# First query and key tiles of three attention branches made in the gate stage, and the threshold rows spread over three merges

## What is computed

```python
def token_mixer(x, w_in, b_forget, sinks, w_branch, w_gate, b_gate, w_out):
    ...
    (aq, ak, av, bq, bk, bv, cq, ck, cv, ciq, cik, ciw, dq, dk, dv, df) = jnp.split(x @ w_in, offsets, axis=-1)
    ...
    o_a, _, _ = banded_attention(...)      # window of 128, sinks
    o_b = dilated_attention(...)           # three dilations
    o_c = dsa_attention(...)               # the 256 best keys of each query by an indexer's score
    o_d = forgetting_attention(...)        # a bias from cumulative forget gates
    branches = jnp.stack([o.reshape(b, L, BRANCH_WIDTH) for o in (o_a, o_b, o_c, o_d)], axis=2)
    proj = jnp.einsum('bsnk,nkd->bsnd', branches, w_branch)
    gates = jax.nn.sigmoid(x @ w_gate + b_gate).reshape(b, L, N_BRANCH, D_MODEL)
    merged = jnp.sum(gates * proj, axis=2)
    return merged @ w_out
```

## Time and profile before

| | us |
|---|---|
| median of three runs (2091.12 to 2094.64) | 2093.48 |
| the profiled execution | 2093.97 |
| its span, first to last instruction | 2092.2 |
| TensorE busy | 2060.4 |
| VectorE busy | 1536.4 |
| ScalarE busy | 968.5 |
| GpSimd busy | 937.3 |

### The profile page before, as it was taken

How to read it: one execution, slowest core, us unless ns; L and a number is a source line. 1 busy time by engine, 2 the same in 40 slices (tenths; PEclk the granted TensorE clock), 3 DMA queues, 4 the chain that set the end, 5 groups by cost and what they waited for, 6 DMA issues and landing times.

```text
span 2092.2 us, 28999 instructions
## 1 busy us (share of the span) xinstructions
PE 2060.4 (98%) x10382; PEld 1727.0 (83%) x10382; DVE 1536.4 (73%) x2549; ACT 968.5 (46%) x1740; POOL 937.3 (45%) x796
## 2 busy tenths in 40 slices
PE   9999999999999999999999999999999999999998
PEld 7788888888888888888888888888788888888887
DVE  8678887777686666797785666668877777775668
ACT  5543334566615556615635666523433333344540
POOL 4287752333322223324523333524756565645651
PEclk9999999999999999999999999999999999999999
DMA  4233323110042111230031000441566665558862
GB/s 132 72 111 110 101 91 62 31 31 21 26 152 64 50 32 51 75 100 28 22 121 31 21 21 11 141 161 61 180 181 203 191 192 161 171 189 310 270 215 92
DMA packets 197373, 224.26 MB, mean 107 GB/s; under 512 B 25704, under 2 KB 149608, under 8 KB 197232
## 3 DMA queue, kind: packets, MB, share of 16 engines
q1 hardware_dynamic: 194320, 212.43, 32.7%
q10 hardware_dynamic: 2912, 10.00, 1.3%
HBM read 164.17 MB, written 58.23 MB: 106 GB/s over the span
## 4 chain that ended last, share of the span: by engine, by line
PE 87%; DVE 7%; issue 2%; ACT 2%; POOL 1%; DMA 0%; DVEq 0%; ACTq 0%; POOLq 0%
PE pair L1359 13%; PE pair L927 13%; PE pair L911 7%; PE pair L1225 7%; PE obank L1359 5%; PE pair L1388 5%; PE obank L1021 4%; PE chunk L1000 4%; PE pair L1318 3%; PE chunk L1388 3%; PE obank L1225 3%; PE pair L972 3%; PE pair L973 3%; PE pair L1271 2%; PE obank L1388 2%
## 5 line engine op out<-in xcount | busy, mean ns | idle before, releaser
L2175 POOL TENSOR_TENSOR w_lo<-w_raw,w_hi 128x1024 fp32r<-128x1024 f32 x64 | 159.5, 2492 | 311.1 <-ACT w_hi L1652 311.0
L1675 ACT ACTIVATE pt_hi<-chunk 128x512 fp32r<-128x512 f32 (+1 forms) x272 | 150.8, 555 | 179.2 <-PE chunk L1000 177.8
L2578 DVE TENSOR_TENSOR pt_lo<-chunk,pt_hi 128x512 fp32r<-128x512 f32 (+1 forms) x272 | 173.2, 638 | 80.1 <-ACT pt_hi L1675 75.7
L2230 POOL TENSOR_SCALAR prob<-prob,att 128x256 f32<-128x256 f32 (+4 forms) x172 | 118.1, 696 | 198.5 <-DVE att L2514 198.2
L927 PE MATMUL pair<-act_hi,w_hi 128*128 128x512 f32 x432 | 186.4, 432 | 2.5 <-DVE heads L2519 2.3
L927 PE MATMUL pair<-act_hi,w_lo 128*128 128x512 f32 x432 | 170.0, 393 | 0.0
L927 PE MATMUL pair<-act_lo,w_hi 128*128 128x512 f32 x432 | 169.4, 392 | 0.0
L2399 DVE TENSOR_SCALAR_CACHE_REDUCE o_top<-score,stat 128x384 uint8<-128x384 f32 (+1 forms) x186 | 167.0, 941 | 0.5
L1021 PE MATMUL obank<-pt_hi,heads 128*128 128x256 f32 (+1 forms) x568 | 148.4, 285 | 0.6 <-DVE pt_lo L2578 0.6
L1777 ACT ACTIVATE prob<-prob,att 128x257 f32<-128x257 f32 (+6 forms) x172 | 120.5, 702 | 39.3 <-DVE att L2504 38.0
L1021 PE MATMUL obank<-pt_lo,heads 128*128 128x256 f32 (+1 forms) x568 | 138.6, 281 | 0.0
(11 more groups left out here) (489 smaller groups left out, 5932.5 us busy)
## 6 DMA issues: line engine op xcount, KB each, us to landing
down_sums<-dn_sums SPq DMA_DIRECT2D x40, 512.0 KB, 6.4
w_raw<-in_w_in SPq DMA_DIRECT2D x37, 512.0 KB, 3.8
gates<-o_t SPq DMA_DIRECT2D x22, 512.0 KB, 2.9
up_raw<-in_w_up SPq DMA_DIRECT2D x22, 512.0 KB, 4.8
gate_raw<-in_w_ffn_gate SPq DMA_DIRECT2D x22, 512.0 KB, 6.0
hidden<-gelu_s SPq DMA_DIRECT2D x22, 512.0 KB, 3.3
dn_raw<-down_sums SPq DMA_DIRECT2D x44, 256.0 KB, 4.1
h_in<-down_sums SPq DMA_DIRECT2D x44, 256.0 KB, 4.8
```

The source lines that it names most:

```text
L2175: nc.gpsimd.tensor_tensor(split_into(1, g), w_raw[:, g % 2, 0:kt * cols], split_into(0, g).bitcast(F32), ALU.subtract).then_inc(lo_ready, 1)
L2578: nc.vector.tensor_tensor(pt_lo[:, n % PT_SLOTS, 0:m], t[:, 0:m], pt_hi[:, n % PT_SLOTS, 0:m].bitcast(F32), ALU.subtract).then_inc(chunk_f ...
```

## The change

The six first query and key tiles of D, A and C are appended to the gate tiles (`HEAD_TILES`) and go through the gate stage as three more pairs, copied in place of the sigmoid and stored to `heads_dram`. The gate stage has 14 pairs in place of 11, and `TOPK_GATES` 15 search parts a pair; the whole search, and the counts of larger scores, end there (197 parts). The rows of distances (five parts each) lie in three merges: three rows in B's, two in D's, one in A's.

The projections at the start of D, A and C are gone. In their place is a step `heads`: SP loads V's weights, the two stored tiles into `o_t` rows 0 and 1, D's first two forget biases, and gate tiles 6 and 7 of the branch before, whose homes are now those of tiles 4 and 5. ScalarE and VectorE split the first query and the first key in halves of 512 tokens from `o_t`, then the second ones; the last gate tile of the merge is gated after the first halves (in C after the first two biased scores). TensorE goes from the merge to the V projection, in C to transposes of the stored tile and filler parts (`FIRST_C`), and waits for `first_placed` before the scores that need a half. ScalarE's split of the next weights moves from behind the merge and the projections to between the first two exponentials (in C behind its query splits).

```diff
-TOPK_GATES = {1: 2, 6: 2, 2: 2, 5: 2, 7: 2, 3: 2, 4: 2}
-TOPK_MERGE = {B: (2, 3), D: (1, 2), A: (0, 1), C: (0, 0)}
-TOPK_FIRST = {("k", D): 7, ("q", D): 6, ("k", A): 5, ("q", A): 5}
-SEARCH_PARTS = 191
-DISTANCE_PARTS = 6
+TOPK_GATES = {1: 3, 6: 2, 2: 2, 5: 2, 7: 2, 3: 2, 4: 2}
+SEARCH_PARTS = 191 + NSC
+DISTANCE_PARTS = 5
+MERGE_ROWS = {B: 3, D: 2, A: 1}
+MERGE_PARTS = {B: (8, 2), D: (4, 1), A: (3, 1)}
...
 
-BESIDE_C = (((0, 0), (0, 2), (1, 1), (1, 1), (2, 2), (3, 0), (3, 1), (6, 0), (6, 2), (8, 1),
+BESIDE_C = (((0, 0), (3, 0), (3, 1), (6, 0), (6, 2), (8, 1),
              (10, 1), (11, 2), (12, 2), (14, 0), (17, 2), (18, 2), (20, 2), (21, 1),
              (21, 2)),
...
 EARLY_GATES = {NKT - 3: 4, NKT - 2: 5, NKT - 1: 7}
-FIRST_C = 4
+FIRST_C = (4, 5)
 
 FILLER_GATES = [(B, 1), (B, 2), (B, 3)]
 STORED_GATES = {B: range(1, NKT), A: range(1, NKT), D: range(1, NKT), C: range(1, NKT - len(EARLY_GATES))}
-GATE_TILES = [(br, dt) for br in BRANCH_ORDER for dt in STORED_GATES[br] if (br, dt) not in FILLER_GATES]
+HEAD_TILES = [(what, br) for br in BRANCH_ORDER[1:] for what in ("q", "k")]
+GATE_TILES = [(br, dt) for br in BRANCH_ORDER for dt in STORED_GATES[br] if (br, dt) not in FILLER_GATES] + HEAD_TILES
 NGATE = len(GATE_TILES) // 2
 assert len(GATE_TILES) == 2 * NGATE
...
     for nb, br in enumerate(BRANCH_ORDER):
-        if br == C:
-            out += [("kv_c",)]
-        if br == A:
-            out += [("k", A, 0)]
-        out += [("q", br, 0)]
-        if br in (B, D):
-            out += [("k", br, 0)]
+        out += [("q", br, 0), ("k", br, 0)] if br == B else [("heads", br)]
         out += [("v_c",)] if br == C else [("v", br, 0)]
         out += [("attn", br, pr) for pr in range(PAIRS)]
         out += [("osplit", br), ("merge", br, nb == 0)]
...
-            tile = prob if n % 2 or n == NGATE - 1 else w_raw
+            tile = prob if n % 2 else w_raw
...
+            if tile not in HEAD_TILES:
+                return w_tile(w_gate[0], tile[0] * D_MODEL + tile[1] * P, P)
+            what, br = tile
+            return w_tile(w_in[0], Q_COL[br] if what == "q" else CK if br == C else K_COL[br], P)
+
+        def tile_kept(tile):
+
+            return heads_dram[HEAD_TILES.index(tile)] if tile in HEAD_TILES else gates_dram[tile]
...
+        def first_head(what):
+
+            return o_t[:, 0 if what == "q" else 1, :]
...
-            return dt % 2 if br == FINAL and dt >= 4 else dt % GATE_HOMES
+            if br == FINAL:
+                return dt % 2 if dt >= 4 else dt
+            return dt if dt < GATE_HOMES else dt - 2
...
-                    fill(FIRST_C)
+                    fill(FIRST_C[0])
+                    pe.wait_ge(first_placed, placed_first(br, 1))
                     scores(br, pr, 0)
                     scores(br, pr, 1)
+                    fill(FIRST_C[1])
...
+                        if p == 0 and br != B and u in (4, 8):
+                            pe.wait_ge(first_placed, placed_first(br, u // 4 + 1))
...
                         pe.wait_ge(chunk_free, chunk_base[1])
+                        if pr == 0 and merge_tiles.n:
+                            pe.wait_ge(merge_free, merge_tiles.n)
...
-                if merge_tiles.n and kind in ("q", "k", "kv_c", "outproj"):
+                if merge_tiles.n and kind in ("v", "v_c", "outproj"):
                     pe.wait_ge(merge_free, merge_tiles.n - 1)
-                elif merge_tiles.n and kind in ("v_c", "attn"):
-                    pe.wait_ge(merge_free, merge_tiles.n)
...
+                    if step[1] != B:
+                        pe.wait_ge(first_placed, placed_first(step[1], 1))
                     scores(step[1], step[2], 0)
...
-                    pe.wait_ge(pair_free[1], tiles[1].n)
-                    transpose_tokens(staged)
+                    pe.wait_ge(heads_loaded, 32 * len(BRANCH_ORDER[1:]))
+                    transpose_tokens(first_head("k"))
...
+            def load_heads(br):
+
+                at = BRANCH_ORDER.index(br) - 1
+                if at == 0:
+                    sp.wait_ge(merge_free, 4)
+                else:
+                    sp.wait_ge(sum_done, sums_of(BRANCH_ORDER[at]) + 4)
+                for what in ("q", "k"):
+                    tile = GATE_TILES.index((what, br))
+                    sp.wait_ge(gate_stored[tile % 2], 16 * (tile // 2 + 1))
+                    sp.dma_start(first_head(what), tile_kept((what, br))).then_inc(heads_loaded, 16)
...
-                    sp.wait_ge(merge_free, merge_at(br) + dt - GATE_HOMES + 1)
+                    sp.wait_ge(merge_free, merge_at(br) + dt - 1)
                 else:
-                    sp.wait_ge(sum_done, sums_of(br) + (1 if br == FINAL else dt - GATE_HOMES + 1))
+                    sp.wait_ge(sum_done, sums_of(br) + (1 if br == FINAL else dt - 1))
...
+                if step[0] == "heads":
+                    for source in ring_sources(("v", step[1], 0)) if step[1] != C else ():
+                        load_weights(source)
+                    load_heads(step[1])
+                    if step[1] == D:
+                        forget_bias(0)
+                        forget_bias(1)
+                    for dt in range(GATE_HOMES, NKT):
+                        load_gate_tile(BRANCH_ORDER[BRANCH_ORDER.index(step[1]) - 1], dt)
                 for n, source in enumerate(ring_sources(step)):
-                    if step in (("q", B, 0), ("k", B, 0)):
+                    if step in (("q", B, 0), ("k", B, 0), ("v", D, 0), ("v", A, 0)):
                         continue
...
-                        if n < NGATE - 3:
+                        if n < NGATE - 2:
...
-                            br, dt = GATE_TILES[2 * n + k]
-                            sp.dma_start(gates_dram[br, dt], gate_out[k]).then_inc(gate_stored[k], 16)
+                            sp.dma_start(tile_kept(GATE_TILES[2 * n + k]), gate_out[k]).then_inc(gate_stored[k], 16)
...
+                if tile in HEAD_TILES:
+                    return nc.scalar.activation(dst, src, ACT.Copy)
+                return nc.scalar.activation(dst, src, ACT.Sigmoid, bias=gate_bias_of(*tile))
...
+            def first_heads(br):
+
+                at = BRANCH_ORDER.index(br)
+                act.wait_ge(merge_full, NKT * at)
+                act.wait_ge(heads_loaded, 32 * at)
+                first_half(br, 0)
+
+            def first_half(br, s):
+
+                q_hi(br, 0, 0, first_head("q")[0:HD, half_cols(s)], half_cols(s))
+                k_hi(0, first_head("k")[0:HD, half_cols(s)], cols=half_cols(s))
+
+            def other_heads(br):
+
+                first_half(br, 1)
+                q_hi(br, 0, 1, first_head("q")[HD:P, :])
+                if br != C:
+                    k_hi(1, first_head("k")[HD:P, :])
+                if br == D:
+                    act.wait_ge(merge_free, merge_at(B) + NKT)
+                    spill(NKT - 1)
+                if br == C:
+                    ahead()
...
+                elif kind == "heads":
+                    first_heads(step[1])
+                    if step[1] != C:
+                        other_heads(step[1])
...
+                    other_heads(C)
...
-                    for u in range(2):
-                        exps(step[1], step[2], u)
+                    exps(step[1], step[2], 0)
+                    if step[1] != B:
+                        ahead()
+                    exps(step[1], step[2], 1)
...
-                    else:
-                        ahead()
                     if br == B:
                         for t in SPILLED:
-                            if t > NKT - 4:
+                            if NKT - 4 < t < NKT - 1:
...
-                    split_weights(min(needed + 2, len(ring_list)) - ring.n)
+                    if br == D:
+                        pool.wait_ge(sum_done, sums_of(D) + 2)
+                        for j in range(PROB_SLOTS):
+                            set_sinks(0, j)
+                        pool.wait_ge(sum_done, sums_of(D) + NKT - 1)
+                        make_bias(0)
+                    split_weights(min(needed + (2 if br == FINAL else 1), len(ring_list)) - ring.n)
+                elif step[0] == "heads":
+                    pass
...
+                yield
+                for i in range(FIRST_TOPK, NTOK):
+                    b = i - FIRST_TOPK
+                    own(nc.vector.tensor_scalar(junk[:, 0, 0:(i + 1) * P], score[:, SC_OFF[i]:SC_OFF[i] + (i + 1) * P],
+                                                cand.bitcast(F32)[:, b:b + 1], None, ALU.is_gt, ALU.add,
+                                                accum_out=count[:, b:b + 1]))
+                    if b < NSC - 1:
+                        yield
...
-                    own(nc.vector.tensor_scalar(junk[:, 0, 0:n], s, limit[:, b:b + 1], None, ALU.is_gt, ALU.add,
-                                                accum_out=above[:, b:b + 1]))
-                    yield
...
+                    if b == MERGE_ROWS[B]:
```

(64 more changed lines are left out.)

149 lines of the change are left out of this document (57 added, 92 removed).

## The result

The changed kernel takes **2102.12 us** (median of 6 runs, 2100.00 to 2104.22), the kernel before 2093.32 beside it (6 runs, 2091.12 to 2094.64): a ratio of **1.0045**, 95% interval 1.0034 to 1.0056. It is 8.8 us slower. Forecast were 2093.8 and a range of 2087.5 to 2098.5, so forecast and range both missed.

A forecast was written before the change was run, and what follows sets the result against it. TensorE was taken as the bound, so the kernel ends when its products run out. Products -8.22, new waits +1.8 in D, +2.5 in A, +4.2 in C sum to +0.3: 2093.8 us, range 2087.5 to 2098.5.

The forecast's parts named there:

- Products and gate stage: Products give -8.22 us; three more gate pairs of 19.04 us, VectorE busy 17.9 of each, at no further cost.
- The starts of D and A: Hand-overs: first transposes at 14.95 and 15.05 us after the merge, waits 2.25 and 3.05, net +1.8 and +2.5.
- the clash that was named: Starts of D and A: VectorE's last key split, now reading SBUF, waits until GpSimd's 2.4 us weight split is over.
- C's start: Hand-over without V projection: fifth score at 11.95 us after a 2.65 us wait, eighth at 19.6, net +4.2.
- The small waits that were told behind it: C's start, behind the fifth score's wait: 1.05, 0.6, 0.15 and 0.9 us, before the eighth score.
- The sum: Whole kernel: -8.22 + 1.8 + 2.5 + 4.2 = +0.3 us, forecast 2093.8 us.
- The cross-check of the prediction: Spans at the starts of D, A and C: 56.6 us gained, one more filler part (0.68) counted, 57.1 paid.
- +0.3: Whole kernel: the predicted net change in us, products saved against new waits in D, A and C.
- The cover: Rival at branch starts: V matmuls and filler parts hide more than thought; 2088.2 us at the lows, chance 0.32.
- The weights in C: Rival at C's start: next query weights load late, 4.1 us late with a 9.2 us landing, 2097.9 us; chance 0.12.
- its upper end: Top of the forecast range, 2098.5 us, set to reach to the late weights in C.

The follow-up runs named there:

- e2_busy: Changed kernel with matmuls of no use added, 13 ahead of A's first transposes and 14 ahead of C's fifth score: 2098.08 us.
- e1_filler: Changed kernel with one filler part taken out of the middle of C's first pair and done later: 2098.32 us.

## Why the prediction was wrong

**Products and gate stage: right.** The gate pairs take 19.04 us; VectorE works 17.84 of them where 17.9 were reckoned, so it does not set the pace. No row shows a late tile in a merge, with some luck: ahead of B's first gated tile VectorE spent 11.7 us (636.36 to 648.09) where about 6 were reckoned, and the fifth tile, which needs it, began at 652.54.

**The starts of D and A: right in place and size.** The first transposes came 14.5 and 15.2 us behind the merge (forecast 14.95 and 15.05), with waits of 1.91 and 3.33 (2.25 and 3.05), by the clash that was named. No score wait stands ahead of the first score.

**C's start: right in place, too small.** The fifth score came at 12.6 instead of 11.95, its wait was 3.55 instead of 2.65, and the eighth score came at 21.2 instead of 19.6. The small waits that were told behind it (1.05, 0.6, 0.15, 0.9) shrank to 0.27, 0.17 and 0.23, in front of the sixth, seventh and eighth score, since TensorE ran at half speed through most of them. When it was kept busy they were 0.80 in front of the sixth score, 0.45 in front of the transposes behind it, and 1.11 in front of the eighth.

**The first step that failed: the price of a wait.** The sum took a wait at its length and every stretch at the 1.00 that the earlier trace rows show for full stretches. The prediction shows no row behind a long wait, though the trace of before has one, in A: 1.71 us of waiting, and the clock at 0.50 for 3.41 us from there on (before, timeline of TensorE and table of stretches).

```profile
1028.40 0.79 PE L911 MATMUL pair<-act_hi,w_hi 128*128 128x512 f32 x1 [1.71 <-DVE heads L2519]
...
1028.38:1031.79 3.41, 3.38 (x13) 3.10 (x14) 2.09 (x7) 1.49 (x5) 1.15 (x4) 0.50 0.00 0
```

In A the half clock cost 1.5 us on top of 3.33. At C's start it cost 0.9 (e2_busy); most of what it took there was time that TensorE would have waited anyway. In C's last pair it cost about 2.7, an estimate from 5.86 us busy at 0.50 and steps of 0.43 us for 0.23.

**The second step that failed: the filler part.** The cross-check of the prediction counts "one filler part (0.68) more done" at C's start as a gain, and the sum has no term for what the shifted stream meets further on. The kernel before waits 0.55 us at the last tile already; one place earlier is 2.5 us earlier (3.06 less 0.55), and VectorE's copy comes where it did, behind two biased scores (after, timeline of VectorE):

```profile
1292.13 0.68 DVE L2572 CUSTOM_DVE_ANT_0 aux<-pair,score 128x512 f32<-128x512 f32 x1
...
1292.73 0.69 DVE L2632 COPY early_gates<-pair 128x512 f32<-128x512 f32 x1
```

This cost 3.6 us by the medians, wait and half clock together (e1_filler). It is the largest single miss: of the 9.9 us between +0.3 and +10.2 in the balance, 5.3 stand in C's last pair, 1.9 at A's start, 1.8 ahead of D and 1.5 at C's start.

**Rivals.** The cover did not hold. The weights in C were not late, but by 0.1 us only, where 1.35 were reckoned: their load ended the wait of ScalarE's split at 1116.74, GpSimd was done at 1120.27, and the first filler part began at 1120.37 (after, timelines of ScalarE, GpSimd and TensorE).

```profile
1116.74 1.06 ACT L1683 ACTIVATE w_hi<-w_raw 128x1024 fp32r<-128x1024 f32 x1 [17.65 <-DMA w_raw<-in_w_in]
...
1117.88 2.39 POOL L2235 TENSOR_TENSOR w_lo<-w_raw,w_hi 128x1024 fp32r<-128x1024 f32 x1 [15.50 <-ACT w_hi L1683]
...
1120.37 0.47 PE L942 MATMUL pair<-act_hi,w_hi 128*128 128x512 f32 x1
```

The range missed since its upper end stood on the waits' lengths alone and had nothing for C's last pair.

## What to carry to other kernels

A wait of TensorE can cost the slow stretch behind it on top of its length, as each wait of over 3 us did here, so covers taken away can cost more than the products that they held; before a cover is taken, price the wait at both. When a hand-placed stream of filler work moves by one part, follow it to its last entry: the loss may stand far from the edit. A change whose saving is lost in queue orders can be worth keeping: here the same products with other orders came out 0.16% ahead of the kernel before.

## What the runs showed of the hardware

- In the traces of after and of all these runs each of the 15 waits of 3.04 to 3.59 us is followed by a stretch at 0.50, of 3.41 to 10.24 us. Behind D's wait of 1.91 or 1.92 the clock fell in two of five traces, and behind A's wait of 1.70 or 1.71 in seven of eleven (before among them), with the same products around it; that may be a part of why one kernel's executions differ (granted clock 0.993 to 0.996 and 2100.0 to 2104.2 us in the six of after).
- A VectorE pass with two SBUF inputs holds up GpSimd's normalise too, an operation with one tensor input: 1.84 us for 0.83, and 2.64 for 1.70. The Trainium skill (SBUF — State Buffer, "SBUF: two separate sides") says that whoever starts first keeps the shared ports for its whole instruction; the rows agree, with losses on either engine (GpSimd's split 3.15 for 2.40, VectorE's pass 3.32 for 1.23).
